# Norms at the joints of a two-block transformer kernel: roots, post-norms and the final norm placed elsewhere, last down rows per token tile

## The reference, cut to what matters

```python
def rms_norm(x, g):
    return x * lax.rsqrt(jnp.mean(x * x, axis=-1, keepdims=True) + EPS) * g

def first_block(x, ...):
    h = x
    h = h + even_mixer(rms_norm(h, norm_mix[0]), ...)            # recurrence and attention
    h = h + swiglu(rms_norm(h, norm_ffn[0]), w1, w3, w2)         # hidden 2816
    h = h + odd_mixer(rms_norm(h, norm_mix[1]), ...)             # gated linear attention
    h = h + moe_swiglu(rms_norm(h, norm_ffn[1]), router, ...)    # 8 experts, top 2, hidden 3584
    return rms_norm(h, norm_final)

def second_block(x, ...):
    for l in range(2):
        h = rms_norm(x, ffn1_pre_g[l])
        x = x + 0.5 * rms_norm(swiglu(h, ...), ffn1_post_g[l])   # hidden 2816
        h = rms_norm(x, mix_pre_g[l])
        x = x + rms_norm(hybrid_mix(h, ...), mix_post_g[l])
        h = rms_norm(x, ffn2_pre_g[l])
        x = x + 0.5 * rms_norm(swiglu(h, ...), ffn2_post_g[l])
    return x
```

## Time and profile before

| what | value |
|---|---|
| median of 3 runs | 2492.46 us (2490.64 to 2493.31) |
| the profiled execution's own time | 2492.23 us |
| its span | 2490.5 us |
| mean granted TensorE clock over the span | 0.996 |
| TensorE busy | 2443.8 us, 98%, 14218 matmuls |
| VectorE busy | 2037.4 us, 82% |
| ScalarE busy | 1542.6 us, 62% |
| GpSimd busy | 72.5 us, 3% |
| VectorE's weight splits (L2162) | 1328.9 us, 1122 of 1.221 us |
| ScalarE's weight casts (L1544) | 1144.6 us, 1122 of 1.052 us |
| DMA | 597.30 MB, mean 240 GB/s |

### The profile page before, as it was taken

How to read it: one execution, slowest core, us unless ns; L and a number is a source line. 1 busy time by engine, 2 the same in 40 slices (tenths; PEclk the granted TensorE clock), 3 DMA queues, 4 the chain that set the end, 5 groups by cost and what they waited for, 6 DMA issues and landing times.

```text
span 2490.5 us, 39422 instructions
## 1 busy us (share of the span) xinstructions
PE 2443.8 (98%) x14218; PEld 2091.2 (84%) x14218; DVE 2037.4 (82%) x2967; ACT 1542.6 (62%) x2139; POOL 72.5 (3%) x158
## 2 busy tenths in 40 slices
PE   9999999899999999999999999999999999999998
PEld 8888887788888888888888788889888888898887
DVE  7777766899899999999999877789877877798776
ACT  6754554677778777777787754463544544644543
POOL 9000000000000000000000000000000000000000
PEclk9999999999999999999999999999999999999999
DMA  7466543699999999999999966633566566533663
GB/s 211 145 194 188 167 153 127 222 371 369 356 356 376 366 353 364 374 361 355 364 378 358 347 194 187 191 109 96 179 193 187 176 186 194 144 99 107 206 190 101
DMA packets 481898, 597.30 MB, mean 240 GB/s; under 512 B 21882, under 2 KB 313154, under 8 KB 481760
## 3 DMA queue, kind: packets, MB, share of 16 engines
q1 hardware_dynamic: 478048, 589.47, 70.7%
q0 software_dynamic: 3712, 6.00, 0.8%
HBM read 594.35 MB, written 1.05 MB: 239 GB/s over the span
## 4 chain that ended last, share of the span: by engine, by line
PE 92%; DVE 4%; ACT 2%; issue 1%; DMA 0%; ACTq 0%; DVEq 0%
PE bank L825 25%; PE bank L631 16%; PE bank L851 12%; PE bank L667 12%; PE bank L637 8%; PE bank L616 5%; PE bank L613 2%; PE bank L1493 2%; PE bank L836 1%; PE bank L1191 1%; PE bank L1021 1%; PE bank L772 1%; PE bank L904 1%; PE bank L647 0%; PE bank L1326 0%
## 5 line engine op out<-in xcount | busy, mean ns | idle before, releaser
L2162 DVE TENSOR_TENSOR wlo_ring<-raw_ring,whi_ring 128x1024 fp32r<-128x1024 f32 (+1 forms) x1122 | 1328.9, 1221 | 102.3 <-ACT whi_ring L1544 85.7
L1544 ACT CAST whi_ring<-raw_ring 128x1024 fp32r<-128x1024 f32 (+1 forms) x1122 | 1144.6, 1052 | 163.6 <-DMA raw_ring<-in_od_exp_w_dram 145.4
L631 PE MATMUL bank<-x,whi_ring 128*128 128x512 f32 x1720 | 428.3, 391 | 0.0
L631 PEld LDWEIGHTS bank<-x,whi_ring 128*128 128x128 f32 x1720 | 315.6, 188 | 60.7
L637 PEld LDWEIGHTS bank<-x,wlo_ring 128*128 128x128 f32 x1720 | 220.8, 191 | 8.4
L637 PE MATMUL bank<-x,wlo_ring 128*128 128x256 f32 x1720 | 223.5, 283 | 0.0
L1615 ACT COPY arena<-bank 128x256 f32<-128x256 f32 x110 | 40.9, 372 | 283.0 <-PE bank L637 283.0
L616 PE MATMUL bank<-x,whi_ring 128*128 128x256 f32 (+2 forms) x1024 | 192.6, 289 | 1.6 <-DVE x L2232 1.5
L825 PE MATMUL bank<-whi_ring,xg0hi 128*128 128x512 f32 x448 | 177.7, 397 | 1.4 <-issue 1.4
L825 PE MATMUL bank<-whi_ring,xg1hi 128*128 128x512 f32 x448 | 177.2, 395 | 0.0
L825 PE MATMUL bank<-whi_ring,xg0lo 128*128 128x512 f32 x448 | 174.8, 390 | 0.0
(11 more groups left out here) (534 smaller groups left out, 3438.1 us busy)
## 6 DMA issues: line engine op xcount, KB each, us to landing
raw_ring<-in_od_exp_w_dram SPq DMA_DIRECT2D x672, 512.0 KB, 5.4
raw_ring<-in_ffn_w_gate_dram SPq DMA_DIRECT2D x88, 512.0 KB, 4.0
raw_ring<-in_ffn_w_up_dram SPq DMA_DIRECT2D x88, 512.0 KB, 4.9
raw_ring<-in_ffn_w_down_dram SPq DMA_DIRECT2D x88, 512.0 KB, 3.4
raw_ring<-in_ev_ffn_w_dram SPq DMA_DIRECT2D x66, 512.0 KB, 4.0
raw_ring<-in_w_in_dram SPq DMA_DIRECT2D x42, 512.0 KB, 4.0
raw_ring<-in_od_w_in_dram SPq DMA_DIRECT2D x24, 512.0 KB, 3.9
raw_ring<-in_ev_w_in_dram SPq DMA_DIRECT2D x20, 512.0 KB, 7.1
```

The costliest lines, as they stand in the source:

```text
L631: mm_ = mm(bank[:, :], wh[:, kt, :], X2[:, kt, :, :].rearrange("p a n -> p (a n)"), start=(start and kt == 0), stop=(stop and kt == KT - 1 ...
L1544: nc.scalar.copy(WHI[:, slot, 0:n], RAW[:, slot, 0:n]).then_inc(s["hi_ready"], 1)
L2162: V_.tensor_tensor(WLO[:, slot, 0:n], RAW[:, slot, 0:n], WHI[:, slot, 0:n].bitcast(F32), ALU.subtract)\
```

## The change

**Odd mixer.** VectorE makes `ffn_roots()` first, then copies LRT; `ahead(c0)` is gone, its split comes with `ahead(c0 + 1)`.

**Roots.** `spread_roots` loads ROOT[t], broadcast over 128 columns, as weights and streams IDENT, in the place of ones and DIAG; `ffn_roots` raises diag_ready with ROOT and makes no DIAG. The call of `spread_roots` moves from `up` into `ffn`.

**Final norm.** Behind the experts the raw sum H is turned (`turn_experts`, by halves of tile 1), and `gain` applies the product of norm_final and ffn1_pre0, made once in the even mixer (norm_final gets a row in the table of columns). The final norm's squares, roots and updates of H stand behind these, then the second squares; `ffn_roots(again=True)` multiplies the second root by the first, and FFN 1 of layer 0 takes it after both first `up`s (`late_roots`) and ten fill matmuls. Chunk 3's split is made by `ahead(f1["c0"])` before that, and chunk 4's right behind the roots; ScalarE makes its Silu table load by a scratch instruction ahead of the FFN.

**Ends of FFNs.** The last two tiles' `up`s come first, then `last_downs`: the last three `down`s for token tile 0, then for tile 1. The last tile's hidden has buffers of its own, HIDHI3 and HIDLO3. SyncE, ScalarE and VectorE load and split these chunks in the new order. `out_part` does the same for a hybrid's output: the last three chunks first for tile 0, then for tile 1.

**Post-norm.** Tile by tile: product, mean, root and update of tile 0, then those of tile 1, whose update comes in two halves (half_ready, h_ready).

**Turns.** `turn_plain` is gone; `turn_sums(banks, 9)` takes its place for FFN 2 of both layers and FFN 1 of layer 1, with 3 fill matmuls ahead of tile 0's turn and 9 behind it. Banks come from `turned(phase)`. `turn_norm` fills 4, 12 and 4 matmuls in the place of 10, 5 and 4.

**Output.** Three DMAs in the place of one: tile 0, then the halves of tile 1.

The core of the diff, its indentation reduced, context lines kept where they tell the place:

```diff
-        load(c0 + 3 * F - 1, (c0 + 3 * F - 1) % RING, rows(w2, (F - 1) * P))
+        b = c0 + 3 * F - 7
+        w13(0, F - 2, b, b)
+        w13(0, F - 1, b + 2, b + 2)
+        for i in range(3):
+            load(b + 4 + i, (b + 4 + i) % RING, rows(w2, (F - 3 + i) * P))
...
+sp.wait_ge(s["h_ready"], 2 * 11 - 1)
+sp.dma_start(out[0, 0:P, :], H[:, 0, :]).then_inc(s["out_done"], 16)
+sp.wait_ge(s["half_ready"], 10)
+sp.dma_start(out[0, P:S, 0:512], H[:, 1, 0:512]).then_inc(s["out_done"], 16)
 sp.wait_ge(s["h_ready"], 2 * 11)
-sp.dma_start(out[0].rearrange("(t p) d -> p t d", p=P), H[:, :, :]).then_inc(s["out_done"], 16)
-sp.wait_ge(s["out_done"], 16)
+sp.dma_start(out[0, P:S, 512:D], H[:, 1, 512:D]).then_inc(s["out_done"], 16)
+sp.wait_ge(s["out_done"], 3 * 16)
...
-        last = mm(BANK[4][:, t * P:(t + 1) * P], ONES[:, :], DIAG[:, t, :], start=True, stop=True)
+        last = mm(BANK[4][:, t * P:(t + 1) * P], ROOT[t].broadcast_to([P, P]), IDENT[:, :], start=True, stop=True)
...
+    if not late_roots:
+        spread_roots()
     up(c_ + 2, cs + 2, q + 1, (qs + 1) % 2, False, n)
+    if late_roots:
+        spread_roots()
+        keep_busy(7, 10)
...
-    with pe.Fori(0, T // 2 - 1) as i:
+    with pe.Fori(0, T // 2 - 2) as i:
...
-    c_, t_ = cs + 6 * m, ts + 2 * m
-    down(c_ + 3 * T - 1, cs + 3 * T - 1, t_ + T - 1, (ts + T - 1) % 2, banks, stop=True)
+    c_, q = cs + 3 * T - 7, qs + T - 2
+    up(c_, c_, q, q % 2, False, n)
+    up(c_ + 2, c_ + 2, q + 1, (q + 1) % 2, False, n)
+    last_downs(c_ + 4, ts, T, banks)
+def last_downs(c_, ts, T, banks):
+    for t in range(TT):
+        for i in range(3):
+            tile = T - 3 + i
+            if t == 0:
+                pe.wait_ge(s["lo_ready"], c_ + i + 1)
+                pe.wait_ge(s["hid_ready"], ts + tile + 1)
+            b = (ts + tile) % 2
+            hi, lo = (HIDHI3[:, :], HIDLO3[:, :]) if i == 2 else (HIDHI[:, b, :], HIDLO[:, b, :])
+            wh, wl = WHI[:, (c_ + i) % RING, :], WLO[:, (c_ + i) % RING, :]
+            for a, (x, w) in enumerate(((hi, wh), (hi, wl), (lo, wh))):
+                for h in range(2):
+                    last = mm(banks[t][h][:, :], x[:, t * P:(t + 1) * P], w[:, h * 512:(h + 1) * 512],
+                              start=False, stop=(i == 2 and a == 2), skip_group_check=True)
+            if t:
+                last.then_inc(s["chunk_used"], 1)
+        if t == 0:
+            last.then_inc(s["y_ready"], 1)
...
-    keep_busy(3, 10)
+    nxt("half_ready")
+    keep_busy(3, 4)
     pe.wait_ge(s["h_ready"], nxt("h_ready", 2) - 1)
-    keep_busy(3, 5)
+    keep_busy(3, 12)
...
+    spare = 4 - banks[3]
+    keep_busy(spare, busy // 3)
     pe.wait_ge(s["h_ready"], h - 1)
     for b in range(4):
         turn_block(banks, 0, b)
+    keep_busy(spare, busy)
...
+def turn_experts():
     for b in range(4):
+        if b == 0:
+            pe.wait_ge(s["half_ready"], nxt("half_ready"))
+        if b == 2:
+            pe.wait_ge(s["h_ready"], nxt("h_ready", 2))
+        for t in range(TT):
+            last = turn_block(TURNED, t, b)
+        last.then_inc(s["tp_ready"], 1)
+    nxt("h_ready", 2)
+    nxt("ssq_ready", 4)
...
+        out_part(pos, 0)
+        if pos < KT - 3:
+            out_part(pos, 1)
+    for pos in R(KT - 3, KT):
+        out_part(pos, 1)
...
-    turn_plain(after_experts=(l == 0))
-    ffn(f1)
+    if l:
+        turn_sums(turned(f1), 9)
+    else:
+        turn_experts()
+    ffn(f1, late_roots=(l == 0))
...
-    turn_plain()
+    turn_sums(turned(f2), 9)
...
-    for i in range(4):
+    for i in range(3):
...
-    load_root()
-    ahead(m_chunk(N_GROUPS, 3), LEAD, end)
...
-            if t == TT - 1:
-                act.wait_ge(s["y_mean"], nxt("y_mean"))
-                af(STAT[:, 18 + h:19 + h], STAT[:, 8 + h:9 + h], ACT.Sqrt).then_inc(s["root_of_y"], 1)
+        act.wait_ge(s["y_mean"], nxt("y_mean"))
+        af(STAT[:, 18 + t:19 + t], STAT[:, 8 + t:9 + t], ACT.Sqrt).then_inc(s["root_of_y"], 1)
...
+load_root()
+ahead(m_chunk(N_GROUPS, 3))
+gain("norm_final")
 norm()
 for l in range(2):
     f1, pr, ou, f2 = HY[l]
-    ffn_entry(f"ffn1_pre{l}")
-    ffn(f1)
+    if l:
+        ffn_entry(f"ffn1_pre{l}", turned(f1))
+    else:
+        ahead(f1["c0"])
+        norm()
+        af(SCRATCH_COL, EPS_COL, ACT.Silu)
+    ffn(f1, begun=(l == 0))
...
-        V_.tensor_scalar(DIAG[:, t, :], IDENT[:, :], y, c_, ALU.mult, ALU.mult).then_inc(s["diag_ready"], 1)
-        link(V_.tensor_tensor(ROOT[t], y, c_, ALU.mult))
-        link(V_.tensor_scalar(ROOT_D[t], ROOT[t], D ** -0.5, None, ALU.mult))
+        if again:
+            link(V_.scalar_tensor_tensor(ROOT_D[t], y, c_, ROOT[t], ALU.mult, ALU.mult))
+            V_.tensor_copy(ROOT[t], ROOT_D[t]).then_inc(s["diag_ready"], 1)
+            V_.tensor_scalar(ROOT_D[t], ROOT_D[t], D ** -0.5, None, ALU.mult)
+        else:
+            V_.tensor_tensor(ROOT[t], y, c_, ALU.mult).then_inc(s["diag_ready"], 1)
+            link(V_.tensor_scalar(ROOT_D[t], y, c_, D ** -0.5, ALU.mult, ALU.mult))
...
-    ffn_roots()
-    split(3, m)
+        V_.tensor_tensor(lo, HID[:, b, :], hi.bitcast(F32), ALU.subtract).then_inc(s["hid_ready"], 1)
+    ffn_roots(again=begun)
+    split(4 if begun else 3, m)
...
-        split(3 * j + 4, m)
+        if j == T - 2:
+            split(3 * j + 4, m)
         hidden(j, m)
+    split(3 * T + 1, m)
...
-    ahead(m_chunk(N_GROUPS, 3), LEAD, end)
+            elif t == TT - 1:
+                last.then_inc(s["half_ready"], 1)
...
-        if t == 0:
-            mean(0)
-    mark("gbc_used")
...
+        if t:
+            mark("gbc_used")
+        dve.wait_ge(s["y_ssq"], nxt("y_ssq"))
+        V_.tensor_scalar(STAT[:, 8 + t:9 + t], STAT[:, 4 + t:5 + t], STAT[:, 6 + t:7 + t], EPS,
+                         ALU.add, ALU.add).then_inc(s["y_mean"], 1)
...
+        if t < TT - 1:
+            update(slice(0, D)).then_inc(s["h_ready"], 1)
+        else:
+            update(slice(0, 512)).then_inc(s["half_ready"], 1)
+            update(slice(512, D)).then_inc(s["h_ready"], 1)
...
+    V_.tensor_tensor(colr("norm_final", KT), colr("norm_final", KT), colr("ffn1_pre0", KT), ALU.mult)
...
-    ahead(c0)
+    ffn_roots()
     dve.wait_ge(s["chunk_used"], c0 + 1)
     V_.tensor_copy(LRT[:, :], BANK[q0 % 2][0:16, 0:S]).then_inc(s["bank_free"], 1)
-    ffn_roots()
...
+gain("norm_final")
+ahead(m_chunk(N_GROUPS, 3))
...
-    link(V_.tensor_tensor(STAT[:, 2 + t:3 + t], y, c_, ALU.mult))
-    V_.scalar_tensor_tensor(H[:, t, :], H[:, t, :], STAT[:, 2 + t:3 + t], GBC[:, gi, :], ALU.mult,
...
+    if l:
+        gain(f"ffn1_pre{l}", turned(f1))
+    else:
+        ahead(f1["c0"])
+    ffn(f1, begun=(l == 0))
```

More of the change, by code:

```diff
@@ L655, in up, with down @@
                         by_high(False, True).then_inc(s["chunk_used"], 1)
-                    if first and half:
-                        spread_roots()
-            def down(c_, slot, t_, b, banks, start=False, stop=False):
+            def down(c_, slot, t_, b, banks, start=False):
                 wait(pe, "lo_ready", c_ + 1)
@@ L1507, in _ @@
             even_mixer(EV_PROJ, EV_OUT)
-            turn_sums(TURNED_MID)
+            turn_sums(turned(EV_FFN))
             ffn(EV_FFN)
@@ L2275, in ffn @@
                 gate(0, m)
-                split(4, m)
+                if not begun:
+                    split(4, m)
                 hidden(0, m)
```

124 lines of the change are left out of this document (52 added, 72 removed).

## The result

The changed kernel takes 2477.05 us (median of 4 runs, 2476.37 to 2479.05), the kernel before beside it 2492.89 us; the ratio is 0.9937, with an interval of 0.9925 to 0.9949: 15.8 us less, where 15.0 were forecast.

The account below looks back on a forecast made before the run. TensorE, busy 98% of the span, was taken as the bound, so only joints between stages could move; 2.0 + 5.0 + 2.1 + 1.2 + 1.6 + 3.3 - 0.2 = 15.0 us saved from 2492.46 gave 2477.5, 80% range 2473.5 to 2484.5.

Parts of the forecast that it names:

- Odd mixer: At the odd mixer's roots: TensorE's whole 2.06 us wait at `spread_roots` goes; 2.0 us won (bounds 1.3 to 2.06).
- Experts to first FFN: From experts to first `down`: final norm moves beside the FFN, VectorE's 14.4 us chain bounds; 5.0 us won (2 to 7.5).
- Downs per tile and posts per tile: Stage ends: FFN to hybrid wins 2.1 us over two joints, hybrid to FFN 1.2 over two, FFN to next layer 1.6.
- Rival 2: At stage ends, per-tile post-norms win nothing, as VectorE and ScalarE still split when tile 0 comes: 2482.4 us; chance 0.10.
- E: The moment at which a stage's last matmul has delivered, about 0.2 us behind the start of the fill block after it.
- Sizes at the ends: At FFN ends, tile 0's update ends at E + 0.6 and tile 1's at E + 4.9.
- The output: After the last matmul: earlier post-norms and a store in smaller pieces win 3.3 us together (2.2 to 3.7).
- What I set at nothing: In the long loops between joints: TensorE's work is the same before and after, so nothing is won there.
- Rival 1: At the experts' joint, the final norm beside the FFN wins 1 us instead of 5: 2481.5 us; chance 0.15.
- Rival 3: More than summed: clock and data ready at the experts' joint, turns overlapping further: 2474.5 us; chance 0.12.
- Rival 4: At six joints, less fill and barer waits drop the clock to 1.2 GHz, 3.5 us lost each: 2498.5 us; chance 0.03.
- The 4.3 us of useful work: Useful matmul time at half clock per joint from which the clock's fall was said to decide the outcome.

Follow-up runs that it names:

- run 2: Changed kernel with final norm, turn of the normed H and one pair of roots ahead of the FFN at the experts' joint, as before: 2477.84 us, ratio 0.9936.
- run 3: Kernel before with only ScalarE's scratch table load (`load_root`) and the experts' last ring cast moved behind the join of the branch: 2490.07 us against 2493.82, ratio 0.9984.
- run 6: Changed kernel with both tiles' post-norms interleaved as before, downs per tile, and the kernel before's fill counts: 2484.74 us against 2493.82 for the kernel before, ratio 0.9959.
- run 4: Changed kernel with the last three downs and output chunks chunk by chunk, post-norms still per tile: 2490.48 us, ratio 0.9987 to the kernel before.
- run 8: Changed kernel with the output in one DMA once H is complete: 2479.12 us, ratio 0.9939 to the kernel before.
- run 5: Changed kernel with both tiles' post-norms in the old interleaved order, downs still per tile: 2492.22 us, ratio 0.9995 to the kernel before.
- run 7: Changed kernel without the fill matmuls of `turn_norm`, `turn_sums` and the late roots, waits kept: 2485.44 us, ratio 0.9964 to the kernel before.

## Why the prediction was right, and where it was not

**Odd mixer.** Right, 2.11 for 2.0. The copy and the splits came 0.5 and 0.7 us sooner than I reckoned.

**Experts to first FFN.** The chain was right link by link: 14.3 us from the end of VectorE's entry (1433.04) to the first `down`, where 14.4 were summed; updates 4.57 for 4.6, roots 2.6 for 2.9, the chunk 4 split with its wait 1.7 for 1.4. TensorE's two waits are 0.78 and 1.71, forecast 1.2 and 1.6. The step that failed is the other side of the subtraction: why before took 23.2 us from its sums to the `down`. I saw the half clock and neither of the two table loads at 1427.13 and 1429.59, so I put the whole 5.0 down to the final norm beside the FFN. Runs 2 and 3 give that part 1.8 us, and 3.6 to a line of the diff that I had read as bookkeeping (`load_root()` moved out of `moe_sparse`). The number was right, its reason for a third. It was not luck alone: the time before was read from rows that had the loads in them, and the time after was summed without them. But the sum left them out unseen, and what the new order would have won with the load still inside the branch no run tried.

**Downs per tile and posts per tile.** I costed them together, and together they win 1.4, 0.7 to 0.9 and 2.0 us a joint. Rival 2 is false for the change, but true of either half. Downs per tile with the posts together (run 6) leave the joint where it was, 11.21 against 11.23. Posts per tile without the downs (run 4) make it worse, 12.50. A tile's chain takes 4.1 to 4.4 us on VectorE and two of them run behind one another, so the first has to start 4 us ahead of E; that is what the eighteen matmuls of 4.09 us buy.

**Sizes at the ends.** The five joints came out 0.1 to 0.4 us better each: tile 0's update ended at E + 0.3 instead of E + 0.6, and tile 1's at E + 4.6 instead of E + 4.9 (hybrid: E + 5.8 for E + 6.1). The chain of a tile is as long as summed (2.95 and 1.3; measured 4.2 and 4.3 to the start of what follows), but VectorE began tile 0 at E - 3.95, where I had E - 3.8 and 0.2 more for waits. Of the first hybrid's 0.93 us about 0.25 are unsure: the joint of before took 14.07 and 14.08 us in two profiles and 13.80 in a third, and why is open.

**The output.** 3.41 for 3.3. The last quarter landed 2.5 us behind its issue; my 2.3 and the estimate of 2.6 by the Trainium skill, DMA: Bandwidth & Descriptors, section Anatomy of one DMA, stand on either side of it. That section is about DMAs that GpSimd issues, and these stores are SyncE's, so it was borrowed; its figures come close here all the same. Run 8 divides the term: 2.0 for the split, 1.4 for the posts.

**What I set at nothing.** The FFNs after the experts are 0.1 to 0.2 us longer each, but for the last, and the hybrids 0.1, 0.6 us together. At the hybrids it comes with the parts per tile (130.55 with chunks in order, 130.64 without); at the FFNs it stays with the downs in either order, so it may be the two `up`s that now come first, or the third buffer; neither was tried.

**The experts.** Not in the forecast, and nothing that the change does: their stage took 979.0 to 982.7 us in thirteen profiles of kernels with the same instructions in it. The first profile of the changed kernel has the long end; 2.2 us of it lie in the last group, where the clock fell. The clock is not the whole of it: the 982.20 us of run 6 had the full clock to their end. Why the stage varies stays open. That is why the span moved by 13.2 us and the median by 15.8; the second profile's span moved by 16.2, and the median beside it by 17.2.

**The other rivals.** Rival 1 fell: the first `down` came 5.35 us sooner. Rival 3 (18 us) was near in the joints, which gave 17.1; the longer FFNs and the experts took some back. Rival 4 did not happen, but runs 5 and 7 show it: the joints at which it falls lose 1.5 to 1.6 us by the clock in run 5, behind a stand of 2.9 to 3.1 us, and 0.5 to 2.5 in all without fill, less than the 3.5 that I priced. The 4.3 us of useful work from which I let it decide follow from nothing beside them: at six joints it takes 5.0 us at half clock each to eat the 15. In the changed kernel tile 0's H comes at E + 0.3 to E + 1.7, and TensorE stands there for 1.0 us at most.

## What to carry to other kernels

A reordering whose halves need each other (an early tile, and a consumer that takes tiles one by one) should be costed as halves too: each alone was worth nothing or less. Before a gain is put down to the step that was meant to bring it, the stretch of before has to be explained to the last microsecond; a state load that a branch's end throws away looks like part of the chain. Fill is free only where it ends before the data that the next useful matmul waits for, and at the half clock it lasts longer: a fill count belongs to the wait in front of it, and has to be set anew when that wait changes.
